# Masks added as matrix products, a new order of heads, and forget-gate weights held in the array

## The reference, cut to what matters

```python
A_GROUPS = ((128, 1), (512, 4), (2048, 16))       # (window, dilation), four heads each
...
def dilated_mixer(xn, w_qkv, w_o, cos, sin):
    ...
    for g, (window, r) in enumerate(A_GROUPS):
        ...  # tokens of one residue modulo r are gathered
        o, lse = banded_attention(gather(q), gather(k), gather(v), window // r)
        ...
    alpha = jax.nn.softmax(jnp.stack(lses, axis=0), axis=0)
    ...
def banded_attention(q, k, v, n_back):
    ...
    s = jnp.where(mask[None, :, None], s, NEG)    # NEG = -1e30
    m = jnp.max(s, axis=-1, keepdims=True)
    p = jnp.exp(s - m)
    l = jnp.sum(p, axis=-1, keepdims=True)
    ...
def second_block(...):
    ...
            kvf = rms_norm(h, kv_norm) @ w_kvf    # keys, values, and 16 columns for the gates
            ...
            log_f = jax.nn.log_sigmoid((kvf[..., 2 * B_WIDTH:] + b_f).astype(jnp.float32))
            c_sh = jnp.cumsum(log_f, axis=1)
```

## Time and profile before

| | us |
|---|---|
| median of 3 runs | 3230.66 |
| the runs | 3230.66, 3242.38, 3228.09 |
| the profiled execution, its own time | 3255.82 |
| its span in the trace | 3254.1 |
| TensorE busy | 2985.5 |
| VectorE busy | 1806.9 |
| ScalarE busy | 1418.7 |
| GpSimd busy | 537.9 |
| dilated attention, first score product to the end of the last value product | 1980.1 to 2075.5 |
| gates' job, first product to the first product of the keys | 2581.1 to 2601.3 |

### The profile page before, as it was taken

How to read it: one execution, slowest core, us unless ns; L and a number is a source line. 1 busy time by engine, 2 the same in 40 slices (tenths; PEclk the granted TensorE clock), 3 DMA queues, 4 the chain that set the end, 5 groups by cost and what they waited for, 6 DMA issues and landing times. The chain is left out here.

```text
span 3254.1 us, 37105 instructions
## 1 busy us (share of the span) xinstructions
PE 2985.5 (92%) x14510; PEld 2389.0 (73%) x14510; DVE 1806.9 (56%) x2210; ACT 1418.7 (44%) x1888; POOL 537.9 (17%) x706
## 2 busy tenths in 40 slices
PE   7978899898998799999998599889999999889998
PEld 4856788787885487777775277678887787678887
DVE  4447736346545488888884544455544226455543
ACT  3324526245223388878784223333333225343332
POOL 0005415133101522223222000000000004000000
PEclk8989999898998899999999798699999799999999
DMA  5210201023643499999995720223322211223321
GB/s 195 59 54 1 78 8 53 27 53 101 209 155 117 147 358 365 360 367 375 374 378 212 279 92 1 90 67 103 105 97 71 81 40 53 71 67 97 98 91 52
DMA packets 277405, 455.59 MB, mean 140 GB/s; under 512 B 24656, under 2 KB 206800, under 8 KB 258160
## 3 DMA queue, kind: packets, MB, share of 16 engines
q1 hardware_dynamic: 250832, 398.43, 35.3%
q0 software_dynamic: 26400, 54.79, 4.6%
HBM read 450.77 MB, written 39.08 MB: 151 GB/s over the span
## 5 line engine op out<-in xcount | busy, mean ns | idle before, releaser
L253 DVE TENSOR_TENSOR weight_part<-weights,weight_part 128x2048 fp32r<-128x2048 f32 (+1 forms) x65 | 148.2, 2279 | 166.4 <-ACT weight_part L242 166.4
L1005 ACT ACTIVATE up_room<-banks,tap_columns 128x512 f32<-128x512 f32 x88 | 68.6, 779 | 312.8 <-PE banks L298 312.8
L293 PE MATMUL banks<-hT_r,weight_part 128*128 128x512 f32 x496 | 200.3, 404 | 5.0 <-PEq L846 3.3
L242 ACT ACTIVATE weight_part<-weights 128x2048 fp32r<-128x2048 f32 (+1 forms) x65 | 121.7, 1872 | 175.9 <-PE banks L293 170.3
L1046 DVE SCALAR_TENSOR_TENSOR up_room<-banks,tap_columns,up_room 128x511 f32<-128x511 f32 x88 | 66.0, 750 | 237.3 <-ACT up_room L1005 237.3
L298 PE MATMUL banks<-hT_r,weight_part 128*128 128x512 f32 x496 | 195.8, 395 | 0.0
L671 POOL TENSOR_SCALAR branch_mean<-branch_mean 128x1 f32<-128x1 f32 x20 | 4.4, 222 | 1155.1 <-ACT up_room L665 744.5
L253 DVE TENSOR_TENSOR weight_part_o<-weights,weight_part_o 128x2048 fp32r<-128x2048 f32 (+2 forms) x49 | 106.9, 2182 | 142.2 <-ACT weight_part_o L242 142.2
L293 PE MATMUL banks<-hT_r,weight_part_o 128*128 128x512 f32 x432 | 174.1, 403 | 6.7 <-PEq L110 3.8
L298 PE MATMUL banks<-hT_r,weight_part_o 128*128 128x512 f32 x432 | 170.4, 394 | 0.0
L297 PE MATMUL banks<-h_low,weight_part_o 128*128 128x512 f32 x432 | 169.2, 392 | 0.0
(11 more groups left out here) (721 smaller groups left out, 8927.5 us busy)
## 6 DMA issues: line engine op xcount, KB each, us to landing
weights<-in_w_e_gate SPq DMA_DIRECT2D x44, 1024.0 KB, 16.0
weights<-in_w_e_up SPq DMA_DIRECT2D x44, 1024.0 KB, 13.2
hT<-in_w_e_down SPq DMA_DIRECT2D x44, 1024.0 KB, 14.9
weights<-in_w_up SPq DMA_DIRECT2D x88, 512.0 KB, 5.1
gate_up<-in_w_e_gate SPq DMA_DIRECT2D x22, 1024.0 KB
gate_up<-in_w_e_up SPq DMA_DIRECT2D x22, 1024.0 KB
down<-in_w_e_down SPq DMA_DIRECT2D x22, 1024.0 KB
weights<-in_w_down SPq DMA_DIRECT2D x20, 1024.0 KB, 5.1
```

The lines of the kernel that those rows point to most:

```text
L242: c.nc.scalar.activation(self.parts[n % 2][0][:, 0:z], self.raw[n % RAW_SLOTS][:, 0:z], ACT.Copy).then_inc(self.high_ready, 1)
L253: c.nc.vector.tensor_tensor(low[:, 0:z], self.raw[n % RAW_SLOTS][:, 0:z], high[:, 0:z].bitcast(F32), ALU.subtract).then_inc(self.low_ready, 1)
L293: ins = c.nc.tensor.matmul(out, lhs[0], rhs[0], start=start, stop=False)
L1005: nc.scalar.activation(a[:, f % 2, v], c.ps[:, 2 * (f % 4) + v], ACT.Identity, scale=conv[:, 2, ch:ch + 1], bias=bias[:, ch:ch + 1]).then_ ...
```

## The change

In the dilated attention the masks are no longer added by VectorE. The score product leaves its group open, and a second product adds the mask to it: an identity rounded to the reduced float32 in the array, and the rounded mask streamed, 512 columns for a wide unit and 128 for a narrow one. For this ScalarE makes rounded copies: the identity, the first chunk's band and the diagonal masks ahead of the first unit, the other three bands (written over `band` itself) at steps 1 to 3; a semaphore counts them and TensorE waits for the count between the two products. VectorE now takes a plain maximum of the scores in PSUM, and ScalarE reads the scores from PSUM for the exponential. With that the waits move: a score bank is free after the exponential of unit i-3 (before: after its maximum), and the wait for the transpositions of unit i-3, which free `pr`, goes from VectorE to ScalarE. The order of heads in a chunk becomes 0, 4, 5, 1, 6, 7, 2, 8, 9, 3, 10, 11: one wide unit, then two narrow ones.

In the other stage the gates' job becomes one work: the 16 columns of weights are in the array and 512 tokens are streamed, so that 24 products of 512 columns take the place of 96 products of 16 columns. ScalarE empties 16 x 512 sums into `by_head`, four small transpositions on TensorE (at work 1) bring them back to tokens in partitions, in bank 5, and VectorE reads them from there. As the job now has one work in the place of four, all numbers of `ForgetBeside` shift by three against the jobs; VectorE's first step comes at work 2 (was 5), and ScalarE's exponential and logarithm come at work 3 (was 5, now one key work later). GpSimd waits for two works to be out (was five).

```diff
@@ -360,7 +360,7 @@
...
-def attention(c, units):
+def attention(c, units, roundings):
@@ -379,6 +379,7 @@
...
         left = c.sem("at_left")
+        mask_rounded = c.sem("at_mask_rounded")
         block = s.enter_context(nc.Block())
@@ -391,8 +392,13 @@
...
                     if i >= 3:
-                        pe.wait_ge(maxed, i - 2)
-                    nc.tensor.matmul(scores(i)[:, 0:W], u["q"], u["k"], start=True, stop=True).then_inc(scored, 1)
+                        pe.wait_ge(expd, i - 2)
+                    adds = u["adds"]
+                    last = nc.tensor.matmul(scores(i)[:, 0:W], u["q"], u["k"], start=True, stop=not adds)
+                    pe.wait_ge(mask_rounded, u["masks"])
+                    for n, (lhs, rhs, c0) in enumerate(adds):
+                        last = nc.tensor.matmul(scores(i)[:, c0:W], lhs, rhs, start=False, stop=n == len(adds) - 1)
+                    last.then_inc(scored, 1)
                 if 0 <= i - 2 < U:
@@ -416,10 +422,16 @@
...
         def _(act):
+            for to, frm in roundings[:3]:
+                nc.scalar.activation(to, frm, ACT.Copy).then_inc(mask_rounded, 1)
             for i in range(U):
                 u = units[i]
+                if 0 < i <= len(roundings) - 3:
+                    nc.scalar.activation(*roundings[i + 2], ACT.Copy).then_inc(mask_rounded, 1)
                 act.wait_ge(biased, i + 1)
-                nc.scalar.activation(pr[:, i % 3, 0:u["W"]], pr[:, i % 3, 0:u["W"]], ACT.Exp, bias=nm[:, i % 3:i % 3 + 1],
+                if i >= 3:
+                    act.wait_ge(turned, i - 2)
+                nc.scalar.activation(pr[:, i % 3, 0:u["W"]], scores(i)[:, 0:u["W"]], ACT.Exp, bias=nm[:, i % 3:i % 3 + 1],
                                      scale=DH ** -0.5, accum_out=u["l"]).then_inc(expd, 1)
@@ -428,9 +440,7 @@
...
                     dve.wait_ge(scored, i + 1)
-                    if i >= 3:
-                        dve.wait_ge(turned, i - 2)
-                    nc.vector.tensor_tensor_reduce(pr[:, i % 3, 0:u["W"]], scores(i)[:, 0:u["W"]], u["adds"][0][1], 1.0, 4 * NEG, ALU.add, ALU.max, u["m"]).then_inc(maxed, 1)
+                    nc.vector.reduce_max(u["m"], scores(i)[:, 0:u["W"]], AX).then_inc(maxed, 1)
                     dve.wait_ge(maxed, i + 1)
@@ -527,7 +537,7 @@
...
                     if beside:
-                        beside.pe(pe, i)
+                        beside.pe(pe, i, left)
                     i += 1
@@ -1074,7 +1084,7 @@
...
-    def pe(self, pe, i):
+    def pe(self, pe, i, left):
         t = i // 2
@@ -1104,6 +1114,8 @@
...
         self.bf = c.sb(s, "forget_bias", [P, B_HEADS])
+        self.by_head = c.sb(s, "forget_by_head", [B_HEADS, SEQ])
+        self.turned = c.sem("forget_turned")
         self.landed = c.sem("fox_landed")
@@ -1115,9 +1127,14 @@
...
-    def pe(self, pe, i):
+    def pe(self, pe, i, left):
         c = self.c
-        if i == 8:
+        if i == 1:
+            pe.wait_ge(left, 1)
+            for tile in range(NT):
+                last = c.nc.tensor.transpose(c.ps[:, 5, tile * B_HEADS:(tile + 1) * B_HEADS], self.by_head[:, tile * P:(tile + 1) * P], c.ident[0:B_HEADS, 0:B_HEADS])
+            last.then_inc(self.turned, 1)
+        if i == 5:
             pe.wait_ge(self.ready, 5)
@@ -1127,32 +1144,32 @@
...
         c, fx = self.c, self.fx
-        if i == 5:
+        if i == 3:
             act.wait_ge(self.ready, 1)
...
             c.nc.scalar.activation(fx.e, fx.e, ACT.Ln, bias=1.0).then_inc(self.ready, 1)
-        if i == 9:
+        if i == 6:
             act.wait_ge(self.summed, 1)
...
         c, fx, lf = self.c, self.fx, self.lf
-        if i == 5:
+        if i == 2:
             c.nc.vector.memset(fx.cT[:].bitcast(F32), 0.0)
...
             dve.wait_ge(self.landed, 80)
-            dve.wait_ge(left, NT)
-            c.vlink(dve, c.nc.vector.tensor_tensor(fx.z, lf[:, :, 0:B_HEADS], self.bf[:].unsqueeze(1).to_broadcast([P, NT, B_HEADS]), ALU.add))
+            dve.wait_ge(self.turned, 1)
+            c.vlink(dve, c.nc.vector.tensor_tensor(fx.z, c.ps[:, 5, 0:NT * B_HEADS].rearrange("p (t h) -> p t h", h=B_HEADS), self.bf[:].unsqueeze(1).to_broadcast([P, NT, B_HEADS]), ALU.add))
             c.nc.vector.scalar_tensor_tensor(fx.e, fx.z, -1.0, fx.z, ALU.mult, ALU.max).then_inc(self.ready, 1)
-        if i == 7:
+        if i == 4:
             dve.wait_ge(self.ready, 3)
...
             c.nc.vector.tensor_copy(fx.causal_r[:], fx.tri[:, 2])
-        if i == 11:
+        if i == 8:
             dve.wait_ge(self.parted, 1)
@@ -1214,7 +1231,7 @@
...
             pool.wait_ge(self.cleared, 1)
-            pool.wait_ge(left, NT + 1)
+            pool.wait_ge(left, 2)
             self.prepare(c, pool, 0)
@@ -1506,17 +1523,20 @@
...
                 units = []
+                rounded = [c.rounded(x) for x in (band, mask)] + [c.sb(sa, "identity_rounded", [P, P], F32R)]
+                roundings = [(rounded[2][:], c.ident[:]), (rounded[0][:, 0], band[:, 0]), (rounded[1][:], mask[:])]
+                roundings += [(rounded[0][:, cc], band[:, cc]) for cc in range(1, 4)]
                 for cc in range(4):
-                    for hd in range(A_HEADS):
+                    for hd in [n for wide in range(4) for n in (wide, 4 + 2 * wide, 5 + 2 * wide)]:
                         p0 = DH * (hd % 2)
...
                             W=SEQ if g == 0 else P, q=qT[p0:p0 + DH, hd // 2, cc * P:(cc + 1) * P], k=kT[p0:p0 + DH, hd // 2, keys],
-                            adds=[(c.ident[:], band[:, cc] if g == 0 else mask[:, g - 1], 0)],
+                            adds=[(rounded[2][:], rounded[0][:, cc] if g == 0 else rounded[1][:, g - 1], 0)], masks=2 if cc == g == 0 else 3 + cc,
                             v=[v[:, b, hd * DH:(hd + 1) * DH] for b in (range(NT) if g == 0 else [cc])],
                             out=o[:, cc, hd * DH:(hd + 1) * DH], m=m[:, cc, hd:hd + 1], l=l[:, cc, hd:hd + 1]))
-                attention(c, units)
+                attention(c, units, roundings)
             pair = [c.sb(s, f"oT_{x}", [P, KA, SEQ], F32R) for x in ("high", "low")]
@@ -1567,14 +1587,16 @@
...
                               lambda tile, z: kv[1][:, 4 * z:4 * z + 4, tile * P:(tile + 1) * P])
-                f_job = tokens(kvf, 2 * D, B_HEADS, lambda tile: lf[:, tile, 0:B_HEADS], None)
-                project_heads(c, q_jobs, None, ahead=[f_job[0]] + [tile for tile, _ in k_jobs], given=h, beside=TurnBeside(c, second, len(q_jobs)))
+                f_tile = [(KD, B_HEADS, cols(kvf, 2 * D, B_HEADS))]
+                project_heads(c, q_jobs, None, ahead=[f_tile] + [tile for tile, _ in k_jobs], given=h, beside=TurnBeside(c, second, len(q_jobs)))
...
                 forget = ForgetBeside(c, sa, room, t, lf)
+                f_job = (f_tile, [dict(m=B_HEADS, n=SEQ, out=forget.by_head[:], rope=None, lhs=lambda w, h, k: w[:, k * B_HEADS:(k + 1) * B_HEADS],
+                                       rhs=lambda w, h, k: h[:, k])])
                 project_heads(c, [f_job] + k_jobs + v_jobs, None, given=kv, beside=forget, pool_work=room.early(c), first=forget.sp)
...
```

## The result

The changed kernel takes 3283.14 us (median of four runs, 3276.53 to 3289.64), the kernel before 3233.26 us (median of four, 3228.09 to 3242.38). The ratio is 1.0124, with a 95% interval from 1.0077 to 1.0171: slower, by 50 us where 53 were forecast. The profiled run took 3276.53 us. Two runs of this study, of 3495.77 and 3443.73 us, were slow as a whole, with a mean clock of 0.808 and 0.818, and tell nothing here; the ratios leave them out.

A forecast was written before the change was run, and what follows sets the result against it. TensorE was taken to bound the attention, its clock setting the price. Profiled execution 3255.8, less old attention 95.3, plus new attention 137.5, less 14.5 for the gates' job, gave 3283.5 us; range 3220 to 3290 us.

The forecast's parts named there:

- The clock at the start: Dilated attention: one wide and two narrow scores start too thinly, so TensorE's clock falls within the first 2 to 5 us.
- half the rows: Attention's start: of 1.6 us in which TensorE streams, 1.3 are in half the array's rows, counted as thin work.
- That it doesn't come back: Attention after the fall: the work is too thin to restore the clock, which stays at 0.50 to the stage's end.
- The length of the stage: Dilated attention: 137.5 us at the lower clock, of which 119.6 without masks, less 1.5 for the start at full clock.
- the narrow mask at the lower clock: Attention: each mask product of a narrow unit costs 0.33 us at half clock (0.11 to 0.40).
- The masks at full clock: Attention: 48 mask products, 16 wide at 0.29 us and 32 narrow at 0.16 us, cost 9.8 us.
- Rival 3: Attention: the clock holds and mask products vanish in gaps behind the scores; stage 67 us, execution 3213 us; chance 0.08.
- Rival 1: Attention: the clock holds from start to end; stage 76.8 us, execution 3222.8 us; chance 0.21.
- The even order giving back 2 us at full clock: Attention: mixing wide and narrow units can recover 0.6 us a chunk lost at their passage, 2 us in all.
- The gates' job: The other stage: 24 products of 512 columns for 96 products save 14.5 us, from 12.9 to 16.4.
- The base: Kernel before: profiled execution 3255.8 us lost the attention's clock for two chunks; the median run kept it.
- The chances: Whole kernel: forecast case, clock lost at the attention's start, 0.62; slower 0.69, same 0.23, faster 0.08.

The follow-up runs named there:

- the order alone: The kernel before with only the head order changed to one wide, then two narrow; masks on VectorE, old gates' job: 3283.66 us, ratio 1.0131.
- attention alone: The changed kernel with the old gates' job, so only the attention differs from the kernel before: 3298.58 us, ratio 1.0156.
- late products: The changed kernel with 16 unread products of 512 columns in a row ahead of the attention's 13th unit, nothing added at the start: 3240.68 us, ratio 1.0024.
- the two runs with three wide units first: New gates' job, two wide units pulled to the front: masks on TensorE, seven runs 3223.94 to 3227.87 us, three 3280.19 to 3284.58; masks on VectorE, 3214.74 us.
- the run with three wide ones first: The changed kernel with two wide units pulled to the front, masks on TensorE: seven runs 3223.94 to 3227.87 us, three 3280.19 to 3284.58 us.
- the run with masks in the old order: The changed kernel with the old head order, four wide then eight narrow; mask products and new gates' job stay: median 3244.43 us, eleven runs 3220.98 to 3281.01.

## Why the prediction was right, step by step

**The clock at the start**, the step that decides: the fall was put 2 to 5 us behind the first score and came after 2.9 us; the first transposition was put 3.3 us behind it (1983.4 less 1980.15) and started 3.3 us behind it, after a wait of 0.44 us for which I had 0.45. By their times and mean clocks it fell in all eight runs of the changed attention and in all four of the order alone; in the four traces of this order's start (changed kernel, attention alone, order alone, late products) it fell 2.9, 3.6, 3.5 and 3.5 us behind the first score. Part of the reasoning is shown (one wide and two narrow scores are too little; more work in the same place cures it), part isn't: "a change of rows after each" and "half the rows" were argued, and the second found no support. Nor is the wait the cause by itself: three wide scores without masks have 0.97 us of it and were lost in 3 of 94 runs, three wide ones with masks have none and were lost in 7 or 8 of 21. So that this start is too little is shown, and which property of it is too little stays open.

**That it doesn't come back**: right in every run of this order, and shown from the other side by the late products.

**The length of the stage**, 137.5 us forecast, 136.2 measured, is right by luck, as two errors cancel. Without masks the same order takes 120.6 us (the order alone), where I had 119.6 - 1.5 = 118.1. By the starts of its chunks (1979.04, 2005.22, 2035.42, 2065.62, end at 2099.61) the first chunk took 26.2 us where I had 26.9 - 1.5 = 25.4: the scaled 26.9 should read 27.1, and of the start at full clock 1.6 of the first 2.9 us are waiting. The two in the middle took 30.2 each, as forecast, and the last took 34.0 where I had 32.3. That end, 1.7 us dearer than the old order's, is the larger part of the error. The masks, with their roundings, cost 136.24 - 120.57 = 15.7 us, where I had 19.0 and 0.4. The mis-sized term is the narrow mask at the lower clock: 0.33 us forecast, 1.68 - 1.45 = 0.23 measured, over 32 of them 3.2 us. A narrow mask streams for 0.11 us at this clock, so that 0.12 us of the identity's load show where I had 0.22: about half of it hides. The wide one was right: 4.54 us to the next unit with it (2000.95 to 2005.49), 4.01 without (2020.32 to 2024.33), 0.53 as forecast.

**The masks at full clock**: 9.8 us forecast and 0.4 for the roundings, 9.7 measured between the two runs with three wide units first, which differ in the masks and the waits and roundings that belong to them. Here too errors cancel in part: a group of three costs 0.54 us more with masks, where my terms make it 0.29 + 2 x 0.16 = 0.61, so 16 groups would give 8.6. Part of the rest lies at the start, where the way to the fourth wide score takes 9.1 us with masks and 7.2 without. Rival 3, masks for free, is out. Rival 1 gave 76.8 us for a stage that holds its clock, and the run with three wide ones first, which is another order, took 77.2.

**The even order giving back 2 us at full clock** wasn't measured alone: 67.6 us with masks on VectorE, against the 68.6 us read for blocks, would be 1.0.

**The gates' job**: -14.5 us forecast, -14.4 measured. Its parts: 7.1 us for 5.5 + 1.7 = 7.2; the small transpositions and the turn to them cost 0.5 us as forecast (the keys' second tile is emptied 6.1 us after the first, for 24 products at 0.233 = 5.6); the keys' weights were ready at 2619.95, 2.4 us ahead of need, where I had 0.9 us; the keys' first tile ran at full clock. The clock did fall at its start, at 2615.6, and was back at 2619.0: 3.4 us at half pace, the 1.7 us that I charged.

**The base**: the reading of the three runs before, that some keep the attention's clock and some lose it for a chunk or two, is borne out by the 75 runs of the kernel before: 38 lie between 3223 and 3235 us, 13 between 3239 and 3247 us, 21 between 3252 and 3262 us, two near 3277 us (the one at 3443.73 us is not counted). The steps are 13 us apart, as one chunk at half pace costs 12.9 us. This scatter also moves the median of a comparison, from 3231.9 to 3244.5 us here, whatever is compared with it.

**The chances**: 0.62 for the forecast was low, for twelve runs of twelve lost the clock. I had doubts whether the start was thinner than that of before by enough, and it was.

## What to carry to other kernels

Where a stage is bound by TensorE, look at its first microseconds before its steady state: here a start of one long and two short units lost the clock in every run, and the work behind it, busy as it was, never brought it back by itself. Try the densest units first, or add products that nobody reads; here 12 of them, some 3 us, were worth 55. And an edit that only evens the order must be costed like the others: it was the whole loss, while the masks cost 10 us at full clock (16 at half) and the gates' job gained 14.

## What the runs showed of the hardware

Both levels of the clock can be stable for the same stream of instructions, with TensorE busy without a gap at either; in this stage only a dense stretch (6.0 us of products of 512 columns) moved it up. The start with three wide scores and masks is near the edge: the same program kept the clock in seven runs of ten and lost it in three, so that one kernel gives two times 57 us apart. A profile of one run shows one of them; ten runs show that there are two. And two heads' scores without anything between them overlap in the array (six records in 1.95 us); with a mask product after each, a wide unit of the start takes 1.45 to 1.49 us, and in the run with masks in the old order the first transposition came 4.3 us after the first score, with no wait left for it. This start has more work and no gap, and yet it loses the clock more often than the one without masks. Its rows:

```profile
1979.34 1.09 PE L397 MATMUL banks<-kT,qT 64*128 64x512 f32 x2 [0.73 <-PEq L473]
1980.36 0.50 PE L400 MATMUL banks<-band_r,identity_rounded 128*128 128x512 f32 x1
1980.79 1.12 PE L397 MATMUL banks<-kT,qT 64*128 64x512 f32 x2
...
1983.66 0.60 PE L408 MATMUL banks<-ident,probs 128*128 128x128 f32 x4
```
